# Starting the attention of a mixer chain beside its index selection, with the gate blocks respread

## The reference

```
qa, ka: 4 heads x 2 parts;  ya = softmax(qa0 ka0) v - lam * softmax(qa1 ka1) v, then rms-normed
yb = softmax(q k * scale + cum[q] - cum[k]) v                 (forgetting attention, 4 heads)
yc = exp(log_sigmoid(z) + reversed cumsum of log_sigmoid(-z)) v     (stick-breaking, 4 heads)
score = sum over 8 index heads of relu(iq . ik) * iw;  idx = top_k(score, 64)
yd = softmax(q k * scale over the keys in idx) v              (indexed sparse attention, 4 heads)
g = sigmoid(h @ w_gate + b_gate)                              (4 branches x 1024)
out = (g0 * (ya @ w_a) + g1 * (yb @ w_b) + g2 * (yc @ w_c) + g3 * (yd @ w_d)) @ w_out
```

## Time and profile before

| | |
|---|---|
| median of 3 runs | 4228.78 us (4223.34 to 4234.53) |
| the profiled execution | 4227.75 us |
| its span | 4226.0 us |
| TensorE matmul busy | 3969.2 us (94%) |
| TensorE weight load busy | 3502.0 us (83%) |
| VectorE busy | 3330.0 us (79%) |
| ScalarE busy | 2060.4 us (49%) |
| mean DMA rate | 222 GB/s |

### The profile page before, as it was taken

The page is one execution under the profiler, slowest core; times in us unless marked ns, Lnnn a source line. Parts: engine busy times, 40 slices in busy tenths (PEclk is TensorE's granted clock), DMA queues, the critical chain, the costliest instruction groups (busy, mean ns, idle before and its releaser), DMA issues. The chain is left out here.

```text
span 4226.0 us, 66651 instructions
## 1 busy us (share of the span) xinstructions
PE 3969.2 (94%) x23036; PEld 3502.0 (83%) x23036; DVE 3330.0 (79%) x7634; ACT 2060.4 (49%) x4043; POOL 616.0 (15%) x475
## 2 busy tenths in 40 slices
PE   7989999999999998989999999899989999988998
PEld 5568999989878886769999887688878888887887
DVE  7777999899778887668966677688676888867687
ACT  5334343577334444335567555444365544436544
POOL 0000034222222221001775000000002000000200
PEclk9999999999999999989999999999999999999999
DMA  6335488899999995657899888654445444544544
GB/s 245 105 135 178 156 301 297 273 295 293 367 340 355 355 348 186 231 179 231 218 233 246 280 277 279 199 193 171 126 130 195 169 179 181 178 131 131 195 169 150
DMA packets 409309, 939.84 MB, mean 222 GB/s; under 512 B 52282, under 2 KB 233770, under 8 KB 395450
## 3 DMA queue, kind: packets, MB, share of 16 engines
q1 hardware_dynamic: 353724, 801.85, 56.8%
q0 software_dynamic: 55296, 134.31, 9.9%
HBM read 842.60 MB, written 93.42 MB: 221 GB/s over the span
## 5 line engine op out<-in xcount | busy, mean ns | idle before, releaser
L167 DVE TENSOR_TENSOR w_low__2<-w_raw__2,w_high__2 128x512 fp32r<-128x512 f32 x544 | 361.6, 688 | 122.8 <-ACT w_high__2 L162 98.1
L162 ACT ACTIVATE w_high<-w_raw 128x512 fp32r<-128x512 f32 x576 | 343.0, 625 | 217.7 <-PE side L149 95.2
L167 DVE TENSOR_TENSOR w_low<-w_raw,w_high 128x512 fp32r<-128x512 f32 x576 | 381.7, 686 | 72.6 <-ACT w_high L162 71.1
L147 PE MATMUL hidden<-hT_high__2,w_high 128*128 128x384 f32 (+1 forms) x1280 | 424.8, 332 | 10.5 <-DVE w_low L167 6.7
L148 PE MATMUL hidden<-hT_low__2,w_high 128*128 128x384 f32 (+1 forms) x1280 | 420.1, 328 | 0.0
L149 PE MATMUL hidden<-hT_high__2,w_low 128*128 128x384 f32 (+1 forms) x1280 | 419.7, 328 | 0.0
L162 ACT ACTIVATE w_high__2<-w_raw__2 128x512 fp32r<-128x512 f32 x544 | 322.2, 624 | 115.5 <-DMA w_raw__2<-in_peer_v 59.3
L147 PE MATMUL hidden__3<-hT_high__4,w_high__2 128*128 128x256 f32 x1152 | 326.8, 284 | 0.0
L149 PE MATMUL hidden__3<-hT_high__4,w_low__2 128*128 128x256 f32 x1152 | 323.4, 281 | 0.0
L148 PE MATMUL hidden__3<-hT_low__4,w_high__2 128*128 128x256 f32 x1152 | 323.2, 281 | 0.0
L1161 POOL DMA_INDIRECT scattered_dram<-selected__3,routing_cells x128 | 230.9, 1804 | 158.0 <-DVE selected__3 L1513 94.0
(11 more groups left out here) (1060 smaller groups left out, 11754.9 us busy)
## 6 DMA issues: line engine op xcount, KB each, us to landing
w_raw<-in_peer_u SPq DMA_DIRECT2D x128, 512.0 KB
w_raw<-in_peer_v SPq DMA_DIRECT2D x128, 512.0 KB
w_raw__2<-in_peer_u SPq DMA_DIRECT2D x128, 512.0 KB
w_raw__2<-in_peer_v SPq DMA_DIRECT2D x128, 512.0 KB
carried_raw__2<-in_up SPq DMA_DIRECT2D x44, 1024.0 KB, 5.4
activated_dram<-activated SPq DMA_DIRECT2D x128, 192.0 KB
routing_dram<-routing SPq DMA_DIRECT2D x24, 1024.0 KB
routing_chunk<-routing_dram SPq DMA_DIRECT2D x16, 1536.0 KB
```

What stands on the lines that cost most here:

```text
L147: nc.tensor.matmul(out, lhs[0], rhs[0], start=start, stop=False, skip_group_check=True)
L162: return nc.scalar.activation(high, src, ACT.Copy)
L167: return nc.vector.tensor_tensor(low, src, high.bitcast(F32), ALU.subtract)
```

## The change

Three things change in `mixer_chain`, for both layers. `ATT_AT` goes from `TOP_AT` + 10 to `TOP_AT` + 1, so the attention steps begin at tick 26 and `TICKS` falls from 78 to 69; `RMS_AT` moves with it. The list `units` now has the `b` units of the second tile right behind those of the first, ahead of all `c` and `d` units; the `turn` units keep their places 24 to 31. And `share` gives 2.0 halves per tick to ticks 25 to 34 and 1.05 from tick 35 on, where it gave 2.25 and 0.9. No operation is added or left out.

```diff
--- before.py
+++ after.py
@@ -3058,8 +3058,8 @@
                         out=yT[:, h, t * P:(t + 1) * P])
 
         units = [diff_unit(h, t) for t in range(TT) for h in range(H)]
-        units += [head_unit(name, h, 0) for name in "bcd" for h in range(H)]
-        units += [head_unit("b", h, 1) for h in range(H)]
+        units += [head_unit("b", h, t) for t in range(TT) for h in range(H)]
+        units += [head_unit(name, h, 0) for name in "cd" for h in range(H)]
         units += [turn_unit(h, t) for t in range(TT) for h in range(H)]
         units += [head_unit(name, h, 1) for name in "cd" for h in range(H)]
         U = len(units)
@@ -3073,11 +3073,11 @@
         NR = len(turned_blocks)
         IDX_AT = NR
         TOP_AT = IDX_AT + 8
-        ATT_AT = TOP_AT + 10
+        ATT_AT = TOP_AT + 1
         RMS_AT = ATT_AT + 2 * H + 4
         TICKS = ATT_AT + U + 3
         HALVES = 2 * BLOCKS_IN
-        share = [(0, 1.25), (IDX_AT, 0.25), (TOP_AT, 2.25), (ATT_AT, 0.9)]
+        share = [(0, 1.25), (IDX_AT, 0.25), (TOP_AT, 2.0), (TOP_AT + 10, 1.05)]
         halves, at = [[] for _ in range(TICKS)], 0.0
         for k in range(TICKS):
             at += [x for start, x in share if k >= start][-1]
```

## The result

The changed kernel took **4248.56 us** (median of 9 runs, 4239.23 to 4261.56) against 4227.44 for the kernel before on the same chip (9 runs): ratio 1.0052, 95% interval 1.004 to 1.0063. It is slower, by 21 us, where 4233.9 was forecast and 4247 was the end of the range. The profiled execution after took 4239.23, the lowest of its nine runs, with a span of 4237.5.

A forecast was written before the change was run, and what follows sets the result against it. VectorE was taken to bound the selection ticks and TensorE the attention. Per layer, 12.5 and 11.4 us saved up to step 9 against 14.5 us more afterwards gave +2.0 and +3.1, together +5.1: 4233.9 us, range 4212 to 4247.

The forecast's parts named there:

- Bounds now: Kernel before: VectorE sets the selection ticks 25 to 34, where TensorE waits 9.1 us for keep_group; TensorE sets attention.
- Steps 9 to 42: Later attention steps: ten more halves (12 gate matmuls each) at 1.45 us, so 14.5 us more per layer.
- The burst: Twelve halves of gate matmuls in step 37 take 17.4 us; their weights cost nothing, at most some 2 us.
- Ticks 25 to 34: Selection merged with attention steps 0 to 8: VectorE decides with 54.1 us, against 40.2 us on TensorE.
- The first score: Sign in the changed profile: attention's first score comes 3 to 4 us after the first MAX8, not 45.
- The wait for the logarithm: Tick 28, VectorE waiting for ScalarE's first Ln: 1.6 us instead of 3.5, bounds 0 and 3.5.
- The failing step: Interleaved ticks: ScalarE's own work of 3.2 us per tick is hidden by VectorE's 4 to 8 us.
- the end of the stretch: Tick 34: TensorE runs ahead and step 9 begins 0.8 us ahead of VectorE's end; 0.5 us set against it.
- The slow clock: Rival, chance 0.19: TensorE at 1.2 GHz in ticks 33 and 34, 5 to 7 us per layer, total 4245.
- Spread halves: Rival, chance 0.05: the three halves added in steps 17, 24 and 27 cost nothing, 4.35 us less per layer, 4225.
- Interleaving: Rival of full payment, chance 0.14: VectorE's work fits under TensorE's 40.2 us in ticks 25 to 34, total 4203.
- The total: Sum over both layers: +2.0 and +3.1 us, together +5.1, giving a median of 4233.9 us.

The follow-up runs named there:

- before_with_keep_sooner: The kernel before the change, with only ScalarE's group copy (keep_group) issued one half sooner, at n - 1: 4225.37 us, ratio 0.9991.
- keep_one_sooner: The changed kernel with ScalarE's group copy (keep_group) issued one half sooner, at n - 1 instead of n - 2: 4235.16 us, ratio 1.0017.
- exps_behind_gate: The changed kernel with ScalarE's exponentials and probability copies of the nine interleaved ticks behind the gate work, copy still at n - 2: 4226.27 us, ratio 1.0001.

## Why the prediction was wrong

*Bounds now: half wrong.* "TensorE idles in the first regime, and VectorE sets it" held for the rounds, not for the moment at which attention starts. The 9.1 us of `keep_group` waits were read as slack. before_with_keep_sooner shows that the copy's place had cost 4.4 to 5.5 us of chain per layer. VectorE's 1.55 us wait for the first scores was the sign, and I took it out of a sum instead of asking why it was there.

*Steps 9 to 42: right.* 14.5 us forecast for ten halves; the rest grew from 78.6 to 92.9, 14.4. The burst ran twelve halves in 17.45 us (17.4 forecast) with TensorE never idle, and its weights cost nothing. A gate store did hold ScalarE's copy up for 2.61 us, without a wait on TensorE:

```profile
3208.44 0.47 ACT L3286 ACTIVATE gate_logits<-gate,vectors 128x256 f32<-128x256 f32 x1 [2.61 <-DMA gate_logits_dram<-gate_logits]
```

*Ticks 25 to 34: the work right, the wait missing.* VectorE's lane was put at 54.1 and tick 30 at 7.4 us; VectorE was busy 52.9, and tick 30 took 7.6 (3093.77 to 3101.40). With the copy one step sooner the stretch was 56.1 and 56.9 against 55.4, with ScalarE's exponentials behind the gate work 53.6. The first score came 1.2 us behind the first MAX8, not 3 to 4, which changes nothing in the sum.

*The wait for the logarithm: right.* 1.6 us forecast, 1.5 measured.

*The failing step* is the sentence that ScalarE's own sum in a tick, 3.2 us, is "hidden by VectorE's 4 to 8 us", and with it "the end of the stretch", where TensorE was to run ahead and step 9 to come 0.8 us ahead of VectorE's end. It came 0.9 us behind it. For tick 34 the prediction's own numbers did not even hide the sum: it gave VectorE 3.2 us there and ScalarE 3.2. And a sum of busy times on ScalarE says nothing of what stands behind what. The copy stood behind exponentials that wait for VectorE, TensorE behind the copy, and VectorE behind TensorE: in layer 0, by keep_one_sooner, 1.7 us in tick 27 (with a share of the clock that is open, see below) and 3.3 behind the rounds, the two places where VectorE had least to do. That is 5.0 of the 5.7 us by which 55.4 became 61.1, and 4.4 of 6.0 in layer 1; exps_behind_gate takes out 7.5 and 7.8, more than the whole miss. So the stretch was to be 12.5 and 11.4 us shorter and was 6.8 and 5.5 shorter, and the 14.5 us of the rest were no longer nearly paid for.

*The rivals.* The slow clock was given 4245 at 0.19, near the result, by another mechanism. The granted clock was 1.00 from 3116.80 to step 9 (fourth window above). It did fall earlier. It was 0.83 on average in ticks 26 and 27, 1.00 up to 3074.8 while TensorE waited 4.3 us for the copy and 0.64 from 3076 to 3080, behind that wait. In keep_one_sooner, without the wait, it was 1.00 in tick 27. So the low clock may have a share in VectorE's 1.6 us wait there; no run separates it from the lock. In ticks 28 to 33 it was 0.91, where VectorE decides. Spread halves weren't free: the whole 14.4 was paid, and the rule of the Trainium skill, page "Perfetto Trace Analysis", section "Identifying the Most-Contended Engine", which would have made three of them free, isn't borne out. Interleaving did not pay in full: with TensorE's waits for the copy down to 2.4 us (exps_behind_gate) VectorE was busy 51.4 of 53.6 us. On the advice of the same page, section "Optimization Strategy", that interleaving different regimes may help: here it moves VectorE work that TensorE hid for nothing (14.8 us by the forecast) to where VectorE is the bound, and both interleaved kernels that differ from a late one in `ATT_AT` alone have the longer chain (154.0 against 144.0, 148.6 against 140.0).

*The total.* Two chains of +7.6 and +8.9 give +16.5; the medians differ by 21.1 and the profiled executions by 11.5. For the two profiled executions the trace closes the sum: the first MAX8 came 5.6 us sooner, the code between the two chains took 0.4 us less and the code behind them 1.0 more, which with 16.5 makes 11.5. For the medians the 4.6 us that are left lie within the spread of these stages. For the same reason before_with_keep_sooner, with chains shorter by 9.9 in sum and a median shorter by 4.1, is left as unexplained in its total.

## What to carry to other kernels

For every wait in a trace ask what stands ahead of the releasing instruction in its in-order queue, not only how busy its engine is: a cheap copy behind an instruction that waits for a third engine ties all three into one loop. Idle time of the engine that isn't the bound can still be paid for at the border between two regimes, where it becomes the one that is late. And before interleaving two regimes, compare at an equal number of filler blocks, and ask how much of the stretch the bounding engine leaves free: here one queue entry a step sooner, with two halves in every tick and attention left where it was, took 0.3 to 0.4% off, while the best interleaved kernel, with 4222.58 us, can't be told from the kernel before.

## What the runs showed beyond that

The kernel that is faster than both is late_with_keep_sooner: `ATT_AT = TOP_AT + 10`, share 2.0 then 1.05, copy at n - 1; 4211.85 and 4214.04 us in two sets of runs, where the kernels before took 4229.49 and 4226.35. Unexpected was how far stages outside an edit move: between the end of layer 0's chain and the first MAX8 of layer 1 the same code took 594.6 to 602.5 us over the profiles, more than many effects studied here, while the two sets of late_with_keep_sooner agree on the chain to 0.2 us.
